# A decoder layer on eight cores: 1024-token tiles, fp16, seven-product matmuls, and a channel-major mixer

## What is computed

```python
proj = einsum('bsd,dc->bsc', x, w_in)                 # 1536 columns: pool 512 | u 512 | v 512
xp = proj[..., :512]
zg = gelu(proj[..., 512:])                            # exact gelu
pooled = causal_multiscale_pool(xp)                   # 4 groups of 128 channels: mean of the last
                                                      # 2/4/8/16 tokens minus the token itself
pool_out = einsum('bsgc,gcd->bsgd', pooled, pool_w) * pool_scale
v = layer_norm(v, sgu_ln_g, sgu_ln_b)                 # then, per head and chunk of 128 tokens,
sgu_out = u * (tril(w_s) @ v + b_s)                   # a masked 128x128 product over tokens
mix = concatenate([pool_out, sgu_out]) @ w_out
h = layer_norm(alpha * x + mix)
out = layer_norm(alpha * h + (silu(h @ w_gate) * (h @ w_up)) @ w_down)
```

## Time and profile before

| | |
|---|---|
| median of 3 runs | 2855.4 us (2854.92 to 2857.19) |
| span of the profiled execution, slowest core | 2851.5 us |
| spans of the 8 cores | 2845.8 to 2851.5 us |
| TensorE matmuls (PE) | 2584.2 us busy, 91% |
| VectorE (DVE) | 1488.5 us, 52% |
| ScalarE (ACT) | 943.8 us, 33% |
| GpSimd (POOL) | 50.3 us, 2% |
| DMA | 373.41 MB, mean 131 GB/s |

### The profile page before, as it was taken

How to read it: one execution, slowest core, us unless ns; L and a number is a source line. 1 busy time by engine, 2 the same in 40 slices (tenths; PEclk the granted TensorE clock), 3 DMA queues, 4 the chain that set the end, 5 groups by cost and what they waited for, 6 DMA issues and landing times.

```text
span 2851.5 us, 37398 instructions; the slowest of 8 cores (2845.8 to 2851.5 us)
## 1 busy us (share of the span) xinstructions
PE 2584.2 (91%) x13300; PEld 1212.3 (43%) x13300; DVE 1488.5 (52%) x2500; ACT 943.8 (33%) x1300; POOL 50.3 (2%) x67
## 2 busy tenths in 40 slices
PE   3588999999999999999999999999999999999996
PEld 1243444444444444444444444444444444444442
DVE  1543554656455554654656555455644656455454
ACT  1232232433324234242433324233332423323220
POOL 2210000000000000000000000000000000000000
PEclk9799999999999999999999999999999999999998
DMA  9999443344434333443343434333443434344244
GB/s 181 130 166 163 135 147 111 118 129 131 133 120 138 115 122 127 140 133 111 126 130 122 141 126 133 109 121 130 143 136 111 138 109 140 129 130 144 88 144 138
DMA packets 153830, 373.41 MB, mean 131 GB/s; under 512 B 57776, under 2 KB 64304, under 8 KB 153648
## 3 DMA queue, kind: packets, MB, share of 16 engines
q1 hardware_dynamic: 98880, 347.91, 38.6%
q0 software_dynamic: 54768, 23.11, 8.0%
HBM read 360.52 MB, written 50.86 MB: 144 GB/s over the span
## 4 chain that ended last, share of the span: by engine, by line
PE 77%; DVE 7%; DMA 6%; ACT 5%; issue 4%; another core or an unknown queue 0%; DVEq 0%; POOL 0%; ACTq 0%; SPq 0%; POOLq 0%
PE ps L582 19%; PE ps L710 18%; PE ps L585 18%; PE ps L380 11%; PE ps L500 7%; DMA sb_wgur<-scr_gu 2%; DMA scr_gu<-w_gate_up 2%; ACT L594 2%; PE ps L272 2%; DMA sb_poolw<-pool_w 1%; DVE sb_silr L596 1%; DVE sb_hr L257 1%; ACT sb_silr L594 1%; ACT L246 1%; DVE sb_sgr L475 1%
## 5 line engine op out<-in xcount | busy, mean ns | idle before, releaser
L582 PE MATMUL ps<-sb_hT,sb_wgur 128*128 128x512 bf16 x2816 | 676.7, 384 | 21.1 <-DMA sb_wgur<-scr_gu 21.1
L585 PE MATMUL ps<-sb_hT,sb_wgur 128*128 128x512 bf16 x2816 | 669.3, 381 | 0.0
L710 PE MATMUL ps<-sb_wdnr,sb_aT 128*128 128x512 bf16 x2816 | 638.6, 379 | 10.5 <-PE ps L710 1.8
L596 DVE SCALAR_TENSOR_TENSOR sb_silr<-sb_silr,ps 128x512 f32<-128x512 f32 x352 | 240.1, 682 | 482.0 <-ACT sb_silr L594 481.5
L585 PEld LDWEIGHTS ps<-sb_hT,sb_wgur 128*128 128x128 bf16 x2816 | 277.2, 98 | 337.8 <-issue 10.1
L582 PEld LDWEIGHTS ps<-sb_hT,sb_wgur 128*128 128x128 bf16 x2816 | 273.1, 99 | 342.2 <-issue 34.2
L710 PEld LDWEIGHTS ps<-sb_wdnr,sb_aT 128*128 128x128 bf16 x2816 | 267.8, 98 | 345.0 <-issue 43.3
L380 PE MATMUL ps<-sb_win,sb_xTr 128*128 128x512 bf16 x1536 | 357.8, 391 | 60.3 <-DVE sb_xTr L280 58.0
L594 ACT ACTIVATE sb_silr<-ps 128x512 f32<-128x512 f32 x352 | 210.1, 597 | 433.5 <-PE ps L585 405.7
L594 ACT ACT_TABLE_LOAD x150 | 192.4, 1283 | 447.0 <-PE ps L585 445.6
L599 DVE SCALAR_TENSOR_TENSOR sb_aT<-sb_silr,ps 128x512 bf16<-128x512 f32 x352 | 242.2, 688 | 64.0 <-DVE sb_silr L596 62.4
(11 more groups left out here) (55 smaller groups left out, 1351.1 us busy)
## 6 DMA issues: line engine op xcount, KB each, us to landing
sb_wgur<-scr_gu SPq DMA_DIRECT2D x352, 512.0 KB, 4.0
sb_wdnr<-scr_dn SPq DMA_DIRECT2D x160, 512.0 KB, 4.4
sb_xr<-x SPq DMA_DIRECT2D x64, 512.0 KB, 3.9
out<-sb_hr SPq DMA_DIRECT2D x64, 512.0 KB, 5.7
scr_gu<-w_gate_up POOLq DMA_DIRECT2D x44, 256.0 KB, 26.6
sb_wdnr<-scr_dn SPq DMA_DIRECT2D x32, 256.0 KB, 4.1
scr_dn<-w_down POOLq DMA_DIRECT2D x10, 512.0 KB, 48.9
sb_win<-w_in POOLq DMA_DIRECT2D x1, 3072.0 KB, 34.8
```

What stands on the lines that cost most here:

```text
L582: ins = t.matmul(ps[:, bg, :], lhsT=wgur[:, s, k, 0:128], rhs=hT[:, k, :], start=(k == 0), stop=(k == 7))
L585: ins = t.matmul(ps[:, bu, :], lhsT=wgur[:, s, k, 128:256], rhs=hT[:, k, :], start=(k == 0), stop=(k == 7))
L596: S.task("dve", lambda v: v.scalar_tensor_tensor(out=silr[:, q, :], in0=silr[:, q, :], scalar=1.0, in1=ps[:, bg, :], op0=ALU.add, op1=ALU. ...
L710: ins = t.matmul(ps[:, bd[b], :], lhsT=aT[:, k, b * 128:(b + 1) * 128], rhs=wdnr[:, s, kk, :], start=(k == 0), stop=(k == NJ - 1))
```

## The change

Nearly the whole kernel is written anew.

- Tiles have 1024 tokens (`T`), so there are 8 (`NT`). fp16 takes the place of bf16. The host passes x a second time, transposed (`xT`), and weights already laid out in the kernel's blocks, in fp32.
- **Channel-major mixer.** v is projected token-major (8 groups of 8 matmuls), u and the pooled part channel-major (16 groups of 8). Pooling is a running sum by `tensor_tensor_scan` over 1024 tokens and one more VectorE operation. `pool_w` and `pool_scale` are multiplied into `w_out` once (`setup_pe`). The gating product gives channel-major output directly, and its bias is prepared once (`Bsg`).
- **Norms.** The row sum comes from `accum_out` of the residual additions, the sum of squares from ScalarE's Square with `accum_out`, and the reciprocal root from GpSimd's `pow`. z (the normalised h without gain) is made on ScalarE, transposed, and gain and bias are applied when it leaves PSUM; the fp32 h gets its affine separately (`ln1_affines`).
- **Strassen (Winograd form), gate-up**: a 2x2 scheme over token halves (512 each), channel halves and gate/up, with seven products of 4 matmuls for each of 22 j. The sums of h (T1 to T4) are made per tile, those of the weights once, at tile 0. Silu is now ScalarE's `Silu`.
- **Strassen, down**: seven phases of 44 matmuls over token halves, d_ff halves and output column halves; sums of the activations are made on VectorE during the phases. Tile 0 uses a plain product (352 matmuls); prepared weights are written to scratch after it (`dn_prep`).
- **Order.** Program order of TensorE is as written: gate-up(t), down(t), out(t+1), in(t+2) with z and transposes of t+1 inside. All other engines' and queues' order is chosen by a list scheduler at build time (`Sched.schedule`), by earliest start in its model and then by due time. TensorE no longer waits for itself.
- Weights pass through one ring (seven slots of 2048 elements per partition; in gate-up four of 3584). `w_in` and `w_out` are streamed too. XS holds xT and, in gate-up, the scratch s1, s2, s4, l1, l2.

The diff, cut to its core:

```diff
-NMT = NBLK // 4
+T = 1024
+NT = TOK // T
...
+    def build(self, eng_sems, dma_sems):
...
+                for d, raw in self.deps[t].items():
+                    if self.eng[d] == e and self.kind[d] == "op" and self.kind[t] == "op" and e == "pe":
+                        continue
...
+        def load_x(mt):
...
+                S.dma("pool", Xv[:, :, half * 512:(half + 1) * 512], xT_d[mt, :, :, half * 512:(half + 1) * 512],
+                      writes=x_keys(half), nbytes=2 << 20)
...
+        def row_slot(mt, b):
+            if b >= 4:
+                return b
+            return b if mt % 2 == 0 else 8 + b
...
+        def ln_stats(row, s, out16, out16_keys):
+            nm, ssq, ve, rs = (st[:, row, c:c + 1] for c in (2, 3, 4, 5))
+            ts(nm, st[:, row, 0:1], st[:, row, 1:2], -1.0 / D, ALU.add, ALU.mult,
+               [("st", row, 0), ("st", row, 1)], [("st", row, 2)], 0.12)
+            act(out16, H[:, s, :], AF.Square, hk(s) + [("st", row, 2)], out16_keys + [("st", row, 3)],
+                A1(D, 1, 1), bias=nm, accum=ssq)
+            ts(ve, ssq, 1.0 / D, EPS, ALU.mult, ALU.add, [("st", row, 3)], [("st", row, 4)], 0.3, eng="pool")
+            tt(rs, ve, nhalf[:, 0:1], ALU.pow, [("st", row, 4), "nhalf"], [("st", row, 5)], 0.8, eng="pool")
+
+        def ln_affine(row, s, gB, bB, gk, bk_):
+            stt(H[:, s, :], H[:, s, :], st[:, row, 2:3], gB[:], ALU.add, ALU.mult,
+                hk(s) + [("st", row, 2), gk], hk(s), 1.27)
+            stt(H[:, s, :], H[:, s, :], st[:, row, 5:6], bB[:], ALU.mult, ALU.add,
+                hk(s) + [("st", row, 5), bk_], hk(s), 1.28)
...
+            sl = [fetch_in(mt, 0), fetch_in(mt, 1)]
+            for b in range(8):
+                vmm(b, sl)
+            if mt == 0:
+                setup_pe()
+            if prev is not None:
+                ln1_z(prev, 0)
+                transposes(prev, 0)
+                ln1_z(prev, 1)
+            for c in range(4):
...
+            if prev is not None:
+                transposes(prev, 1)
+            for g in range(4):
...
+                S.task("dve", lambda v, g=g, w=w, init=init: v.tensor_tensor_scan(
+                    out=yv, data0=xp[:, g, 16:1040], data1=xp[:, g, 16 - w:1040 - w], initial=init,
+                    op0=ALU.add, op1=ALU.subtract),
+                    reads=xpk(g, 0, 1040) + ([("ylast", g)] if odd else []), writes=yk, dur=2.2)
...
+            for half in range(2):
+                for h in range(4):
+                    sgu(h, half)
...
+            if half == 1:
+                for a, b in ((0, 2), (2, 4)):
+                    d = D2(1024)
+                    tt(hTv("T1", a, b), hTv("T3", a, b), hTv("B11", a, b), ALU.subtract,
...
+                if mt == 0:
...
+                    for i, c in ((0, 0), (4, 1024)):
+                        S.dma("pool", ring[:, gw(s, i): gw(s, i) + 1024], w_gu_d[j, :, c:c + 1024],
+                              writes=bkk(i, 2), nbytes=1 << 19)
...
+                if name == 1:
+                    start(j)
+                    prod(j, 0, "B11", xb, True)
+                    act(s1, ps[:, xb, :], AF.Copy, [], sk(s1o, 2048), A1(512), excl=bk(xb))
+                elif name == 2:
+                    prod(j, 1, "B21", zb, True)
+                    tt(s1, ps[:, zb, :], s1, ALU.add, sk(s1o, 2048), sk(s1o, 2048), D1(512), excl=bk(zb))
+                    act(l1, s1, AF.Silu, sk(s1o, 2048), sk(l1o, 1024), A1(512))
+                elif name == 6:
+                    prod(j, 2, "T2", xb, False)
+                    act(s2, ps[:, xb, :], AF.Copy, [], sk(s2o, 2048), A1(512), excl=bk(xb))
+                elif name == 5:
+                    prod(j, 3, "T1", xb, False)
+                    act(s4, ps[:, xb, :], AF.Copy, [], sk(s4o, 2048), A1(512), excl=bk(xb))
+                elif name == 7:
+                    prod(j, 4, "T3", yb, True)
+                    tt(a2, ps[:, yb, :], s4, ALU.add, sk(s4o, 2048), a2k, D1(512), excl=bk(yb))
+                elif name == 3:
+                    prod(j, 6, "B22", xb, False)
+                    act(l2, ps[:, xb, :], AF.Silu, [], sk(l2o, 1024), A1(512), excl=bk(xb))
+                    tt(a2, a2, l2, ALU.mult, a2k + sk(l2o, 1024), a2k, D2(512))
+                elif name == 4:
+                    prod(j, 5, "T4", yb, False)
+                    tt(a1, ps[:, yb, :], s2, ALU.add, sk(s2o, 2048), a1k, D1(512), excl=bk(yb))
+                    tt(a1, a1, l1, ALU.mult, a1k + sk(l1o, 1024), a1k, D2(512))
+            for c in range(NJ + 1):
+                for name, dj in ((1, 0), (5, 1), (2, 0), (7, 1), (6, 0), (3, 1), (4, 1)):
...
+            for c, i in phase(0, (aR, "a"), A11, XB, True):
...
+                if c == 0 and i == 3:
+                    for f0, f1 in KSPLIT:
+                        asum(E1, (hT, "hT"), ("a", A21), A22, ALU.add, f0, f1)
+                    for f0, f1 in KSPLIT:
+                        asum(A21, (aR, "a"), ("a", A11), A21, ALU.subtract, f0, f1)
+            for f0, f1 in KSPLIT:
+                asum(A11, (aR, "a"), ("hT", E1), A11, ALU.subtract, f0, f1)
+            for c, i in phase(1, (aR, "a"), A12, YB, True):
...
+            for c, i in phase(4, (aR, "a"), A11, XB, False):
...
+            for i in range(4):
+                ln2(mt, 4 + i)
+            for c, i in phase(2, (aR, "a"), A12, XB, False):
...
+        for mt in range(NT):
+            gu = gu_products(mt)
+            dn = dn_plain(mt) if mt == 0 else dn_strassen(mt)
+            for _ in gu:
+                next(dn)
+            drain(dn)
+            if mt + 1 < NT:
+                out_stage(mt + 1)
+                if mt + 2 < NT:
+                    load_x(mt + 2)
+                    in_stage(mt + 2, mt + 1)
+                else:
+                    for half in range(2):
+                        ln1_z(mt + 1, half)
+                        transposes(mt + 1, half)
+                ln1_affines(mt + 1)
+                if mt == 0:
+                    dn_prep(0)
```

More of the change, by code:

```diff
@@ L36, in __init__ @@
         self.last_write = {}
         self.reads = {}
[L38 to L50 removed]
+        self.out_dmas = []
```

1343 lines of the change are left out of this document (714 added, 629 removed).

## The result

The changed kernel takes 2471.9 us (median of four runs, 2463.4 to 2479.9), beside 2855.5 us for the kernel before on the same chip: a ratio of 0.866 (95% interval 0.863 to 0.869). The prediction was 2350 us in a range of 2285 to 2500. The sign and the range held; the point is 122 us too low, and the time lies outside the 2290 to 2400 of the main forecast (chance 0.62), in the 2400 to 2500 that were given to turns bound by another engine (0.18). The rest of this text is about those 122 us.

What follows compares the result with a forecast made beforehand. TensorE's own stream was taken to bound the kernel. Work 2201, first matmul 20, front 25, turns 56, last tile 22 and tail 20 give 2344 us of span; with 4 around it 2348, predicted as 2350, range 2285 to 2500.

Steps and rivals of the forecast that it cites:

- main forecast: Whole kernel: turns lose 2 to 12 us each, giving 2290 to 2400 us; chance 0.62.
- TensorE's work: Whole kernel: 10,004 large matmuls at 0.2158 us and 768 small at 0.055, 2201 us against 2502 before.
- to the first matmul: Kernel start: loading half of xT and two chunks of w_in takes 20 us (15 to 35).
- waits and slow clock of the front: Start and tile 0: all waits and the slow clock at the start cost 25 us (10 to 80).
- turns: Between one tile's last down phase and the next gate-up: small stalls only, 8 us per tile, 56 in all.
- last tile's norm: After tile 7's out-projection, no in-stage covers the norm: about 22 us of bare TensorE (15 to 35).
- tail: After the last matmul: the final rows of the second norm and their store take 20 us (16 to 28).
- I take 0.5, 28 us: GpSimd, each tile: 56 one-column operations for the reciprocal root, taken at 0.5 us each, 28 us.
- Rival 1: Turns are bound by VectorE, GpSimd or ScalarE: 20 us lost per tile, 2430 us, or 2480; chance 0.18 for 2400 to 2500.
- waits of TensorE for GpSimd's pow: Sign in the profile: such waits over 5 us per tile would show the forecast wrong.
- rival 2: Front is bound by the casting weight loads: 58 us more over tile 0's gate-up, 2405 us; chance 0.09 alone.
- rival 3: Whole kernel: denser fp16 stream lowers the granted clock; 2590 us at 0.9, gain gone at 0.81; chance 0.06.

Runs made afterwards that it cites:

- e1: Changed kernel with five buffers instead of two for the gelu of v: 2383 us, ratio 0.834 to the kernel before.
- e2: Changed kernel with v's two one-column operations moved from GpSimd to VectorE, square root left out: 2396 us, ratio 0.839 to the kernel before.
- e11: Changed kernel with each row's first affine of the first norm held until v's last GpSimd power: 2454 us, ratio 0.862 to the kernel before.
- e6: Changed kernel with 21 of tile 0's 22 stores of prepared gate-up weights left out: 2443 us, ratio 0.856 to the kernel before.
- after: The changed kernel itself, against which the experiments are set: 2471.9 us, ratio 0.866 to the kernel before.
- e3: Changed kernel with the one-column operations of v and both large norms moved from GpSimd to VectorE: 2440 us, ratio 0.855 to the kernel before.
- e16: Changed kernel with five gelu buffers and, in tile 0 alone, the pooled section before the u section: 2444 us, ratio 0.857 to the kernel before.
- e10: Changed kernel with five gelu buffers, 32-byte scheduler keys, and v's one-column operations on VectorE: 2376 us (two executions).

## Why the prediction was near, and where it was off

The account of the profiled execution, by the prediction's terms (us; measured from the starts above, each against its work):

| term | predicted | measured |
|---|---|---|
| TensorE's work (measured: what the other terms leave) | 2201 | 2207 |
| to the first matmul | 20 | 28.8 |
| waits and slow clock of the front | 25 | 66 |
| turns | 56 (8 a tile, seven) | 141 (six: 26, then 23 each) |
| last tile's norm | 22 | 16 |
| tail | 20 | 19 |
| span | 2344 | 2477.6 |

**TensorE's work** was right: 608 matmuls of fp16 gate-up in 130.9 us, 0.215 each, as bf16. (10,008 and 768 matmuls at the prediction's prices are 2202 us; the rest is small waits, most of them in the last tile.) Of the 374 us between the two profiled spans it gives 295; the other 79 are lost time, 349 before (2851.5 - 2502.2) and 271 after, where 143 were predicted.

**The turns**, +85 us, are the step that failed. It is the term "In all I take 8 us lost per tile, between 2 (every chain covered) and 18". VectorE's load in the turn came out near the sum (72.8 us measured, 68 predicted), but by luck: the 20 us of the first norm's affines, "put off into gate-up" in the prediction, are in it, and a scan, three gating operations and part of the second norm are not. The prediction's 74.3 us for the turn also names the last down phase but holds only the 320 matmuls of out and in. The down projection was sized well: its sums at 0.42 us per 512, the row above, just fit behind 88 matmuls, and no wait shows. What was wrong is the chain of v, priced only by load. Its GpSimd operation was taken as a constant ("I take 0.5, 28 us"), and the affines as standing elsewhere. The mean is 0.44 to 0.93, the load 15%; but beside 1.27 us affines it lasts up to as long as they do or longer (1.60 for a power), the affines also stand in VectorE's queue ahead of z, and the chain has two buffers. Five buffers take the wait away (e1), GpSimd out of it or the affines behind it nearly so (e2, e11). Rival 1 named the engines and gave 2430 to 2480, by summing operations at 0.84; the time came out there. Its reason was only half right: neither engine is full, a chain through four engines is. That the stated range held is owed to this rival's share of it, not to the forecast. The sign "waits of TensorE for GpSimd's pow" of over 5 us per tile was the right one to name, only that the wait appears under ScalarE's name, two steps on.

The prediction also said that the mixer's chains "now have a whole stage of 64 matmuls (13.8 us) between their links". That holds for z and the gating; it overlooked that the bank of a v block is freed by gelu, and gelu's buffer by z.

**The front**, +41 and +9: 10.5 us of wait at 96 us for pooling and gating of tile 0, the one out-projection with nothing over its scans (2.3 us each; the range 1.3 to 2.6 was right); and 28 us in tile 0's gate-up on the profiled core, of which e6 shows that it is the sum of loads and stores. That is rival 2's place at half its price. It makes core 5 the slowest, 2477.6 us, where the dies' medians are 2455.6; on the other cores it is 4 to 16 us. The first matmul came at 28.8 instead of 20. The DMA engines were full meanwhile (share 1.01 over the first 50 us), probably because both halves of x and w_in's chunks were in flight together; no run tests it.

**The clock**, rival 3: in after not. In stretches without idle time after tile 0 it is 1.00, and its dips follow idle time at the turns; that is a term the sum had not, 1 to 2 us a tile. But e3, e11 and e16 show stretches of 0.78 to 0.94 with next to no idle time of TensorE, and in e16 it takes some 65 us (52 of span, and the 13 that it was ahead of e1 at tile 1). The price in the prediction was of the right form. What brings the lower clock on stays open: e10, with the least idle time at its turns of the other kernels, ran at 0.99 to 1.00 between 500 and 2300 us. The Trainium skill ("TensorE: Matmul & The Clock Gate", the warning on the peak-current limiter) gives 13/16, 0.81, for a die with three or more dense cores. Stretches of 0.81 do occur here (e3 at 560 to 610), but most dense stretches run at 1.00 with all eight cores at work (e1's 1068 to 1347, say), which doesn't agree with the rule as a forecast; the measurement decides.

**Last tile and tail** were right within their bounds. In the sum, all low ends give 2275, not 2276, which changes nothing.

The best version of these is the changed kernel with five gelu buffers: 2383 us, 33 us from the point predicted. Its turns cost 8.9 us a tile (282.6 - 273.7) where 8 were predicted; of the rest, some 8 are the first matmul (27.5) and most of what is left the front.
